# Order of products around an attention loop: a convolution gate ahead of it, a gate's products inside it, layer norm's rows one product earlier

## What is computed

```python
h = rmsnorm(x, mix_norm[i])
z = h @ w_in[i]
zq, zk, zv, zc, zg = [z[..., offs[j]:offs[j + 1]] for j in range(len(SPLIT_SIZES))]
q = partial_rope(rmsnorm(zq.reshape(B, S, N_Q_HEADS, HEAD_DIM), q_norm[i]), cos, sin)
k = partial_rope(rmsnorm(zk.reshape(B, S, N_KV_HEADS, HEAD_DIM), k_norm[i]), cos, sin)
a = sliding_window_attention(q, k, v, sinks[i]) @ attn_proj[i]
ca, cb = jnp.split(zc, 2, axis=-1)
u = ca * jax.nn.sigmoid(cb)
u = causal_depthwise_conv(u, w_dw, b_dw)            # 31 taps
c = jax.nn.silu(layernorm(u, conv_ln_g[i], conv_ln_b[i])) @ conv_proj[i]
ga, gb = jnp.split(zg, 2, axis=-1)
merged = jax.nn.sigmoid(ga) * a + jax.nn.sigmoid(gb) * c
x = x + merged @ w_out[i]
```

## Time and profile before

| | us |
|---|---|
| median of 3 runs | 1984.6 (1984.23 to 1985.56) |
| profiled execution | 1983.71 |
| its span, first to last instruction | 1981.9 |
| TensorE busy in it | 1958.4 |
| VectorE busy | 1208.9 |
| ScalarE busy | 848.9 |
| granted TensorE clock, mean | 0.997 |

### The profile page before, as it was taken

How to read it: one execution, slowest core, us unless ns; L and a number is a source line. 1 busy time by engine, 2 the same in 40 slices (tenths; PEclk the granted TensorE clock), 3 DMA queues, 4 the chain that set the end, 5 groups by cost and what they waited for, 6 DMA issues and landing times. The chain is left out here.

```text
span 1981.9 us, 26230 instructions
## 1 busy us (share of the span) xinstructions
PE 1958.4 (99%) x10250; PEld 1599.3 (81%) x10250; DVE 1208.9 (61%) x1702; ACT 848.9 (43%) x1268; POOL 16.3 (1%) x31
## 2 busy tenths in 40 slices
PE   9999999999999999999999999999999999999998
PEld 6888888888677888788888888777888788888887
DVE  6667565589899645554434367797564456544534
ACT  6544343434777353533313255652654442222222
POOL 0000000000000000000000000011000000000000
PEclk9999999999999999999999999999999999999999
DMA  7889887454333553333333332421143323323231
GB/s 253 297 296 299 288 287 259 165 187 173 128 112 117 183 194 110 109 107 96 96 96 96 91 105 85 118 75 30 49 144 108 105 85 106 97 96 96 96 103 68
DMA packets 82090, 277.52 MB, mean 140 GB/s; under 512 B 9352, under 2 KB 11912, under 8 KB 81968
## 3 DMA queue, kind: packets, MB, share of 16 engines
q1 hardware_dynamic: 80816, 274.47, 42.1%
q10 hardware_dynamic: 1152, 1.38, 0.2%
HBM read 242.70 MB, written 32.52 MB: 139 GB/s over the span
## 5 line engine op out<-in xcount | busy, mean ns | idle before, releaser
L345 PE MATMUL ps<-Hh,whi 128*128 128x512 f32 x1464 | 577.5, 394 | 3.1 <-ACT P L1265 2.1
L349 PE MATMUL ps<-Hh,wlo 128*128 128x512 f32 x1464 | 570.6, 390 | 1.2 <-DVE wlo L1773 1.2
L346 PE MATMUL ps<-Hl,whi 128*128 128x512 f32 x1464 | 569.7, 389 | 0.0
L1080 ACT CAST whi<-raw 128x1024 fp32r<-128x1024 f32 (+3 forms) x352 | 350.0, 999 | 376.7 <-PE ps L349 337.9
L1773 DVE TENSOR_TENSOR wlo<-raw,whi 128x1024 fp32r<-128x1024 f32 (+3 forms) x294 | 338.8, 1157 | 184.1 <-ACT whi L1080 177.6
L345 PEld LDWEIGHTS ps<-Hh,whi 128*128 128x128 f32 x1464 | 274.8, 188 | 68.1 <-issue 4.8
L349 PEld LDWEIGHTS ps<-Hh,wlo 128*128 128x128 f32 x1464 | 274.8, 188 | 59.6 <-DVE wlo L1773 1.9
L346 PEld LDWEIGHTS ps<-Hl,whi 128*128 128x128 f32 x1464 | 275.0, 188 | 58.1 <-issue 2.2
L1889 DVE SCALAR_TENSOR_TENSOR cacc<-upad,gains,cacc 128x512 f32<-128x512 f32 x232 | 160.2, 745 | 0.8
L1839 DVE SCALAR_TENSOR_TENSOR x<-ps,x 128x512 f32<-128x512 f32 x79 | 54.6, 691 | 155.6 <-PE ps L349 155.6
L1815 DVE TENSOR_TENSOR scr<-ps,Rt 128x512 f32<-128x512 f32 x92 | 63.3, 688 | 54.8 <-PE ps L349 40.2
(11 more groups left out here) (384 smaller groups left out, 2820.1 us busy)
## 6 DMA issues: line engine op xcount, KB each, us to landing
raw<-in_w SPq DMA_DIRECT2D x369, 512.0 KB, 4.0
low_parts<-lo SPq DMA_DIRECT2D x58, 512.0 KB, 4.6
wlo<-low_parts SPq DMA_DIRECT2D x58, 512.0 KB, 3.3
raw<-in_w SPq DMA_DIRECT2D x16, 384.0 KB, 3.1
raw<-in_w SPq DMA_DIRECT2D x17, 256.0 KB, 2.6
out<-y SPq DMA_DIRECT2D x8, 256.0 KB, 2.0
x<-in_x SPq DMA_DIRECT2D x5, 256.0 KB, 6.3
raw<-in_w SPq DMA_DIRECT2D x8, 128.0 KB, 2.0
```

The source lines that it names most:

```text
L345: e.matmul(out, h[:, kk, :], a, start=part != "last" and k + kk == 0, stop=False)
L346: e.matmul(out, h[:, kk, :], c, start=False, stop=False)
L349: ins = e.matmul(out, lo[:, kk, :], a, start=False, stop=done)
L1080: e.copy(whi[i % WS][:, 0:n], raw[i % RAWS][:, 0:n]).then_inc(*act.tick("whi", ("whi", i)))
```

## The change

`fill` loses `ca`, `cb` of tile 4 and gets `gb` 2 and 3 at its end. Tile 4 is gated ahead of the loop, as tiles 1 to 3 are, with 14 taps beside it, so every later tap of the list comes 14 places sooner. `gb` 2 is pinned; its multiply on VectorE stays behind the loop. The rows of the layer norm with the centring and squares come one product sooner.

```diff
-        fill = [(w, j) for j in range(4, 8) for w in ("ca", "cb")] + [("ga", j) for j in range(8)] + [("gb", 0), ("gb", 1)]
+        fill = [(w, j) for j in range(5, 8) for w in ("ca", "cb")] + [("ga", j) for j in range(8)] + [("gb", j) for j in range(4)]
...
# tensor_program
-            for j in range(1, 4):
+            for j in range(1, 5):
                 gated(j, 0)
                 gated(j, 1)
...
-                gemm(("gb", j), "w_in", 0, 8, [(4352 + 128 * j, 128)], Hh, Hl, "mix")
+                gemm(("gb", j), "w_in", 0, 8, [(4352 + 128 * j, 128)], Hh, Hl, "mix", pin=j == 2)
...
             pv(len(groups) - 1)
-            gate_b(2)
+            ring.append(bank_of["gb", 2])
             for j in range(8):
                 gemm(("ap", j), "attn_proj", 0, 8, [(128 * j, 128)], aoh, aol, "ao")
-                if j == 3:
+                if j == 2:
                     mean_row("ln_mu", "conv_sum", pin=True)
-                if j == 7:
+                if j == 6:
                     ring.append(bank_of["R", "ln_mu"])
                     mean_row("ln_r", "sum", "lnv", 7, pin=True)
-            for j in range(3, 8):
+            for j in range(4, 8):
                 gate_b(j)
...
# scalar_program
-                s = scr[j % 3] if j < 4 else scr[3 + j % 2]
+                s = scr[j % 3] if j < 5 else scr[3 + j % 2]
...
-            for j in range(1, 4):
+            for j in range(1, 5):
                 after(("cb", j))
                 sigmoid_gate(j)
             after("v")
             act.wait_ge("gemm", "v")
-            act.wait_ge("cb_u", 3)
+            act.wait_ge("cb_u", 4)
...
-            after(("gb", 2))
+            after(("gb", 3))
             for j in range(4, 8):
                 gate_a(j)
             for j in range(8):
                 after(("ap", j))
-                if 4 <= j < 7:
-                    for i in range(3 * j - 12, min(3 * j - 9, 8)):
+                if 3 <= j < 6:
+                    for i in range(3 * j - 9, min(3 * j - 6, 8)):
                         act.wait_ge("xc", i)
                         squares("lnv", i, upad[:, i, 32:544])
-            for j in range(3, 8):
+                if j == 6:
+                    root_row("ln_r")
+            for j in range(4, 8):
                 after(("gb", j))
-                if j == 3:
-                    root_row("ln_r")
...
# vector_program
-                conv(2 if 1 <= j < 4 else 0)
+                conv(2 if 1 <= j < 5 else 0)
...
-            for j in range(1, 4):
+            for j in range(1, 5):
                 after(("ca", j))
                 conv(6 if j > 1 else 0)
                 after(("cb", j))
...
-                elif what == "gb":
+                elif what == "gb" and j != 2:
                     gate_b(j)
...
-            after(("gb", 2))
             gate_b(2)
             conv(7)
             for j in range(8):
                 after(("ap", j))
-                if j == 7:
+                if j == 6:
                     add_square("lnv", 7)
                 gate_a(j)
-                if j < 3:
-                    conv(7 if j < 2 else 248)
-                if 4 <= j < 7:
-                    for i in range(3 * j - 12, min(3 * j - 9, 8)):
+                if j < 2:
+                    conv(7 if j < 1 else 248)
+                if 3 <= j < 6:
+                    for i in range(3 * j - 9, min(3 * j - 6, 8)):
                         center(i)
                         if i > 1:
                             add_square("lnv", i - 1)
-            for j in range(3, 8):
+            for j in range(4, 8):
                 after(("gb", j))
                 gate_b(j)
```

More of the change, by code:

```diff
@@ L1335, in scalar_program @@
                 after(("ap", j))
-                if 4 <= j < 7:
-                    for i in range(3 * j - 12, min(3 * j - 9, 8)):
+                if 3 <= j < 6:
+                    for i in range(3 * j - 9, min(3 * j - 6, 8)):
                         act.wait_ge("xc", i)
                         squares("lnv", i, upad[:, i, 32:544])
-            for j in range(3, 8):
+                if j == 6:
+                    root_row("ln_r")
+            for j in range(4, 8):
                 after(("gb", j))
-                if j == 3:
-                    root_row("ln_r")
-                for i in range(3 * j - 12, min(3 * j - 9, 8)) if j > 3 else ():
+                for i in range(3 * j - 12, min(3 * j - 9, 8)):
                     ln_silu(i)
```

## The result

Twenty runs each gave a median of 1987.39 us (1985.27 to 1989.97) against 1984.24 us for the kernel before: a ratio of 1.0017, 95% interval 1.0011 to 1.0023, that is 3.4 us (2.2 to 4.6). The forecast was +1.1 us, 1985.7, with 1987.5 as its upper end; on the forecast's own base of 1984.6 us the ratio gives 1988.0 us. A second comparison of the same two kernels gave 1.0011 (1.0002 to 1.0020). So the direction was right and the size was not: a third of the first measured cost was forecast, half of the second. Both lie under 0.2%.

A forecast was written before the change was run, and what follows sets the result against it. TensorE was taken as the bound, busy 1958.4 of 1981.9 us, with 4.1 us of waits in the loop's first rounds. Terms -0.65 + 1.75 = +1.1 us took the 1984.6 us median to 1985.7 us; range 1983.2 to 1987.5.

The forecast's parts named there:

- The gate ahead of the loop: Before the loop: gating there makes VectorE 0.3 us later, covered by its 3.09 us standstill before the first rope; cost 0.
- The taps shift by 14: First attention rounds: tile 3's addition to `acc` moves to round 2, so the first three TensorE waits grow together by 0.73 us.
- D(4): Start of VectorE's row maxima (L2009) for group 4: from 521.37 to 522.10 us.
- D(5): Start of VectorE's row maxima (L2009) for group 5: 532.36 us in the profile of before.
- D(6): Start of VectorE's row maxima (L2009) for group 6: from 541.23 to 541.96 us.
- The fourth wait goes: TensorE's 1.32 us wait before round 5's scores vanishes, as no bank is pinned there; gain 0.65 us (0.73 lost, 1.38 won).
- The end of the loop: In `ap` 0, the seventh triple needs the attention's last low part, no longer covered by `gb` 2; TensorE waits 1.75 us.
- D(15): Start of VectorE's row maxima (L2009) for group 15, near the loop's end: 624.38 us before, 622.47 forecast.
- Layer norm's rows: Rows, centring, squares and `gate_a` move one product ahead; the last `acc` addition comes 4 us before it is needed; cost 0.
- Moved work: Two `w_in` products (5.5 us each) change place; no matmul, DMA or vector operation is added or lost: sum 0.
- Slower by the clock: Rival: the wait at the loop's end reaches 3.0 us and the clock falls; +4.7 us, 1989.3 us; chance 0.05.
- Covered end: Rival: VectorE catches up 1.8 us more, so the low part is in time; -0.65 us, 1984.0 us; chance 0.18.

The follow-up runs named there:

- late_low: The changed kernel with two more convolution taps in VectorE's last round, ahead of the last low part: ratio 1.0026 to the kernel before.
- split_at_4: The changed kernel with `ap` 0 and 1 reordered on TensorE: first four k of each, then last four of each. Ratio 1.0004 to the kernel before.
- split_at_4_pad: split_at_4 with three already-met waits more on TensorE at the start: ratios 0.9996 and, run again, 0.9991 to the kernel before.
- b_pad254: The kernel before with 255 already-met waits more on TensorE at the start (254 meant); only profiled once, whole time compared with nothing.

## Why the prediction was wrong

By its steps, in the times of the profile of before (after less 10.60 us):

- **The gate ahead of the loop: right.** The first rope's wait shrank from 3.09 to 2.78 us, the 0.3 us that it was to cover, and the first scores came 10.88 us later, as forecast.
- **The taps shift by 14: right.** D(4) was 522.10 (forecast 522.10), D(5) 533.01 (533.09), D(6) 541.88 (541.96).
- **The fourth wait goes: right.** Gain to the loop's end 0.80 us; forecast 0.65.
- **The end of the loop: right, 0.4 us short.** D(15) was 622.52 (forecast 622.47), the last low part ended at 641.12 (641.06). The seventh triple began at 641.27, 2.09 us after it was wanted; forecast 1.75. TensorE came 0.15 us sooner, the low part 0.06 later, and 0.15 us passed from its end to the matmul. From its first matmul to that of the next product `ap` 0 took 7.75 us, and `gb` 2 had taken 5.58 in its place: 2.17 us, of it 0.72 and 0.96 as waits above. So this stretch gave -0.80 + 2.17 = +1.37, forecast +1.1.
- **Layer norm's rows: right.** The last addition ended at 659.69 and TensorE asked at 664.19 (in after's own time), a margin of 4.5 us where 4 were forecast and the earlier trace rows had 1.5:

```profile
659.00 0.69 DVE L1898 TENSOR_TENSOR acc<-acc,upad 128x512 f32<-128x512 f32 x1
...
664.19 1.02 PE L395 MATMUL ps<-acc,cg 128*128 128x512 f32 x2
```

- **Moved work, "sum 0", is the step that failed**, with "for `ln_r` and all behind it ... Cost 0". The count was right for matmuls, DMAs and vector operations, but it left out the waits, which are instructions too. Two fewer on TensorE moved every later block end by one matmul, and 700 us later that cost about 1 us (0.7 of it in the first pause), a term that stood at nothing. 1.37 - 0.21 + 1.0 = 2.2 us: that is the second comparison's value, and the lower end of the first one's interval. The point value 3.4 of the first is not reached, and the cause of the remaining 1.2 us stays open; scatter in the clock is a candidate that wasn't shown. The row that could have warned was in the profile of before: 3.7 us of L671 ended by "issue", beside no engine's work. With it a range up to 1989 was due.
- **The rivals.** Slower by the clock: the mechanism exists (late_low), the wait was too short for it. Covered end: not with this order, but split_at_4 made it, and got -0.77 us on the stretch, where -0.65 was forecast for that case.

The version with the loop's gain and the early block ends, split_at_4_pad, gave 0.9996 and 0.9991: about 1.3 us below the kernel before, at the edge of what can be measured (both intervals reach 1.0000). Its three waits are tuned to one place of one program, and the next edit ahead of it can undo them.

## What to carry over

When a product that stood between a producer's last result and its consumer is moved away, ask by how much the consumer's first use falls behind; splitting the first two products by k, as in split_at_4, gives the cover back, and its trace shows no new wait. Where a profile shows pauses ended by "issue" in dense small products, any edit ahead of them, even one that only adds or drops a wait, can shift their size by a microsecond: count the instructions, and test with a few met waits at the start before you credit or blame an edit for so little.

## What the hardware showed

- A block of instructions needs its time: from the start of its packet to the first matmul behind the first pause passed 2.2 to 3.0 us in every profile; the packet itself took 0.9 to 1.4 us of that.
- Met waits aren't free on TensorE. In b_pad254 255 of them follow one another from 1.5 to 29.1 us, 0.109 us apart, and hardly differ with the clock (0.108 us at 2.4 GHz, 0.110 at 1.2). The first part runs beside the zero products, so TensorE stood still for 21.9 us:

```profile
1.46 6.00 PE L429 MATMUL ps<-scr 128*128 128x512 f32 x10 [1.46 <-DVE scr L1847]
29.35 0.77 PE L345 MATMUL ps<-Hh,whi 128*128 128x512 f32 x1 [21.89 <-issue]
```

- In every profile TensorE waits once for 3.4 to 3.7 us just ahead of the small products (until 1333.36 us in before). In sixteen of the seventeen it came out of that wait at 1.2 GHz or fell to it within 1.5 us; in after it stayed at 2.4 GHz, behind a wait of 3.6 us, and fell only at 1352.8, with the end of the pause of 2.78 us. In all it ran at 1.2 GHz for 3.4 to 20.5 us of the stretch from 1250 to 1390. The scatter among runs of one kernel goes with it: in the second comparison the runs of before with a mean granted clock of 0.998 took 1982.9 us on average, those with 0.995 took 1986.6.
- The seven chained taps of tile 7 took 5.47 us again, 0.78 us apart, as in the earlier trace rows.
